# Seven block products in both SwiGLU stages, adaLN blocks on GpSimd and ScalarE, and x loaded first

## The reference

```python
# block 1
mod = silu(c) @ ada_w + ada_b                 # 1024 -> 6*1024, "adaLN": shifts, scales, gates
h = modulate(rmsnorm(x, norm1_g), shift1, scale1); proj = h @ w_in    # two attentions, branches, MLP
# block 2, layer A (l = 0): short convolution, then the first SwiGLU stage
# shared keys and values (w_ada_kv), layer B (l = 1): forgetting attention, then the second SwiGLU stage
mod_l = silu(c_2) @ w_ada_2[l] + b_ada_2[l]
y = (silu(h @ gate[l]) * (h @ up[l])) @ down[l]      # gate, up: 1024 x 2816, down: 2816 x 1024
x = layer_norm(alpha * x + gate_mod * y)
```

## Time and profile before

| | us |
|---|---|
| median of 3 runs | 1952.1 |
| the profiled execution's own time | 1950.68 |
| its span | 1948.9 |
| TensorE busy | 1888.5 (97%) |
| VectorE / ScalarE / GpSimd busy | 1291.9 / 814.6 / 466.0 |

### The profile page before, as it was taken

One profiled execution on the slowest core, in us unless ns is written; L12 is line 12 of the kernel. 1 busy time (PEld: TensorE's weight loads), 2 busy tenths in 40 slices (PEclk: granted clock), 3 DMA queues, 4 the chain that ended last, 5 costly groups with the idle time before them and its releaser, 6 DMA issues.

```text
span 1948.9 us, 23971 instructions
## 1 busy us (share of the span) xinstructions
PE 1888.5 (97%) x9600; PEld 1593.4 (82%) x9600; DVE 1291.9 (66%) x1969; ACT 814.6 (42%) x1238; POOL 466.0 (24%) x379
## 2 busy tenths in 40 slices
PE   4999999999999999999999999999999999999997
PEld 3788888887888887888788888877899778999996
DVE  6687655567667645665665555466677676777797
ACT  4677622352222235222522222248677553433333
POOL 4333210121111112001300000025643142445352
PEclk9999999999999999999999999999999999999998
DMA  9522366356565523542455442313211223323331
GB/s 334 153 85 66 113 222 238 120 193 238 211 221 201 188 87 117 186 151 93 168 201 187 173 151 87 108 65 130 71 58 52 87 72 101 109 95 101 108 100 52
DMA packets 134432, 267.65 MB, mean 137 GB/s; under 512 B 4576, under 2 KB 49648, under 8 KB 134321
## 3 DMA queue, kind: packets, MB, share of 16 engines
q1 hardware_dynamic: 129360, 248.59, 37.2%
q0 software_dynamic: 4960, 17.53, 2.5%
HBM read 261.84 MB, written 8.45 MB: 139 GB/s over the span
## 4 chain that ended last, share of the span: by engine, by line
PE 68%; DVE 3%; ACT 3%; POOL 2%; issue 1%; DVEq 0%; POOLq 0%; ACTq 0%
PE ps L720 22%; PE ps L722 21%; PE ps L721 21%; PE ps L880 1%; ACT t L1400 1%; ACT t L1396 1%; PE ps L869 1%; PE ps L858 0%; POOL t L2722 0%; PE ps L897 0%; PE ps L898 0%; PE ps L896 0%; DVE t L1889 0%; DVE t L1874 0%; POOL t L2531 0%
## 5 line engine op out<-in xcount | busy, mean ns | idle before, releaser
L720 PE MATMUL ps<-t 128*128 128x512 f32 (+1 forms) x2720 | 997.0, 367 | 12.1 <-POOL t L2626 5.2
L722 PE MATMUL ps<-t 128*128 128x512 f32 (+1 forms) x2720 | 989.6, 364 | 0.0
L721 PE MATMUL ps<-t 128*128 128x512 f32 (+1 forms) x2720 | 985.8, 362 | 0.0
L720 PEld LDWEIGHTS ps<-t 128*128 128x128 f32 x2720 | 513.2, 189 | 95.3 <-POOL t L2531 5.8
L722 PEld LDWEIGHTS ps<-t 128*128 128x128 f32 x2720 | 512.7, 189 | 84.6
L721 PEld LDWEIGHTS ps<-t 128*128 128x128 f32 x2720 | 513.1, 189 | 79.8 <-issue 1.0
L1810 DVE TENSOR_TENSOR t<-t 128x2048 fp32r<-128x2048 f32 x115 | 267.2, 2323 | 315.7 <-ACT t L1347 315.5
L1347 ACT ACTIVATE t<-t 128x2048 fp32r<-128x2048 f32 x115 | 219.7, 1911 | 465.2 <-PE ps L722 457.6
L1822 DVE CUSTOM_DVE_ANT_0 t<-t 128x1024 f32<-128x1024 f32 x144 | 174.8, 1255 | 6.8 <-DMA t<-in_adakv_t 3.6
L1874 DVE SCALAR_TENSOR_TENSOR t<-ps,t 128x512 f32<-128x512 f32 x184 | 131.7, 748 | 71.4 <-PE ps L722 68.1
L2531 POOL TENSOR_TENSOR t<-t 128x512 fp32r<-128x512 f32 x88 | 115.5, 1330 | 197.1 <-ACT t L1354 196.5
(11 more groups left out here) (196 smaller groups left out, 1894.7 us busy)
## 6 DMA issues: line engine op xcount, KB each, us to landing
t<-in_ada SPq DMA_DIRECT2D x48, 1024.0 KB, 5.9
t<-in_gate SPq DMA_DIRECT2D x22, 1024.0 KB, 5.2
t<-in_up SPq DMA_DIRECT2D x22, 1024.0 KB, 5.2
t<-in_down SPq DMA_DIRECT2D x22, 1024.0 KB, 5.1
t<-in_w_in SPq DMA_DIRECT2D x17, 1024.0 KB, 5.7
t<-in_w_mlp_in SPq DMA_DIRECT2D x16, 1024.0 KB, 5.3
t<-in_w_mlp_out SPq DMA_DIRECT2D x16, 1024.0 KB, 5.1
t<-in_ada_t POOLq DMA_DIRECT2D x13, 1024.0 KB, 6.2
```

The costliest lines, as they stand in the source:

```text
L720: pe.matmul(o, wh, xh, start=first, stop=False)
L721: pe.matmul(o, wh, xl, start=False, stop=False)
L722: return pe.matmul(o, wl, xh, start=False, stop=last)
```

## The change

1. The stage of l = 0 gets the same plan as that of l = 1: `plan_ffn2(l)` for both, 18 "S" slots each. In both stages gate and up slots now alternate, so that one gate tile and one up tile (128x1024 each) do, and the third sums buffer is `spare_b` in place of `csb[1]`. h4 is kept whole (`h4_all`), as h6 was.
2. adaLN blocks 61 to 79 are multiplied by GpSimd (`ada_product`, one 128x2048 `tensor_tensor` each, behind `weight_sums(n + 1)` in its queue) and summed by ScalarE (`ada_sum`, two 128x1024 `Copy` with an accumulator, ahead of the `first product` of the next step). They have two buffers. They fall on slots 75, 76, 77, 79, 80, 81, 83, 84, 85, 87, 88, 89, 91, 92, 93, 95, 96, 97 and 99. The S slots are 79 to 82, 85 to 88, 91 to 94, 97 to 99 and 101 to 103.
3. At the start x is loaded ahead of adaLN blocks 0 and 4; the squares and their sums go ahead of the rest on ScalarE and VectorE; the units of slots 0 and 1 wait for single pieces, and GpSimd does `low(0)` and `low(1)` after two pieces of slot 0.

```diff
+    for w, what in ((gate, "gate"), (up, "up")):
+        for p in range(2):
+            plan_role("A", w, 512 * p, 0, l, what, 0, p)
+    for f in range(4):
+        for p in range(2 if f else 0):
+            plan_role("S", gate, 0, 512 * f + 256 * p, l, "gate", f, p)
+            plan_role("S", up, 0, 512 * f + 256 * p, l, "up", f, p)
+        for hf in range(2):
+            plan_role("A", down, 512 * f, 512 * hf, l, "down", f, hf)
+    plan_role("S", gate, 0, 2560, l, "gate", 4, 0)
+    plan_role("S", up, 0, 2560, l, "up", 4, 0)
+    plan_role("S", gate, 0, 2048, l, "gate", 5, 0)
+    plan_role("C", down, 2560, 0, l, "down4", 4, 0)
+    plan_role("S", up, 0, 2048, l, "up", 5, 0)
+    plan_role("S", gate, 0, 2304, l, "gate", 5, 1)
+    plan_role("S", up, 0, 2304, l, "up", 5, 1)
...
+ADA_FFN = stream_ada()
+for _j in range(ADA_FFN, len(ADA)):
+    _i = _j - ADA_FFN
+    _at = AT_FFN + 2 + _i * 24 // (len(ADA) - ADA_FFN - 1)
+    ADA_BUF[_j] = ("ffn", _i % 2)
+    ADA_LOADS.setdefault(_at - 1 if _i > 1 else AT_FFN, []).append(_j)
+    ADA_SUMS.setdefault(_at, []).append(_j)
...
 (job_unit, TensorE)
+                if n < 2:
+                    on.wait_ge(w_lo_p, "slot", n, u // 2)
+                elif u == 0:
+                    slot_lo(on, n)
                 if u == 0:
-                    slot_lo(on, n)
                     claim(bank)
...
 (ScalarE, start)
-            for i, bank in enumerate((0, 4)): ... row copies
             on.wait_ge(d_cols, "eps")
             for k in range(KT):
                 square("n1", k, x_in[k // 4], "landed")
+            for i, bank in enumerate((0, 4)): ... row copies
+            root("n1", False, rmse)
             for c in range(4):
                 piece(0, c)
-            root("n1", False, rmse)
...
 (ScalarE, ffn2)
+                def ada_sum(j):
+                    on.wait_ge(p_ada, "product", j)
+                    col = ADA[j][2]
+                    for i in range(2):
+                        v = ada_buffer(j)[:, i * D:(i + 1) * D]
+                        ins = act.activation(v, v, ACT.Copy, accum_out=mods[:, col + i:col + i + 1])
+                    ins.then_inc(a_ada.sem, a_ada.up("sum", j))
...
 (VectorE, start)
+            for k in range(1, KT):
+                add("n1", k)
             ada_sum(0)
+            roots("n1", False)
             ada_sum(4)
             two_columns(0)
-            for k in range(1, KT):
-                add("n1", k)
-            roots("n1", False)
...
 (GpSimd)
+            def ada_product(j):
+                on.wait_ge(ada_landed(j), "landed", j)
+                v = ada_buffer(j).rearrange("p (a k) -> p a k", a=2)
+                c = csb[ADA[j][3]][:, :].rearrange("p (a k) -> p a k", a=1).broadcast_to([P, 2, D])
+                pool.tensor_tensor(v, v, c, ALU.mult).then_inc(p_ada.sem, p_ada.up("product", j))
+
             def ffn2(l, site):
-                take(33)
+                for n in sorted(n for n in ROLE if ROLE[n][0] == l):
+                    slot[0] += 1
+                    if in_products(n + 1):
+                        weight_sums(n + 1)
+                    for j in ADA_SUMS.get(n, ()):
+                        ada_product(j)
...
 (SyncE, start)
             sp.dma_start(csb[0][:, :], a["c_b"]).then_inc(c_in[0].sem, c_in[0].up("landed", by=16))
-            ada_load(0)
-            ada_load(4)
             for hf in range(2): ... x
+            ada_load(0)
+            ada_load(4)
             load(0)
```

More of the change, by code:

```diff
@@ L1084, in ffn2, with hidden, down4 @@
+            def ffn2(l, site, h):
+                def hidden(k):
+                    return hidden_t[l][:, 0, k % 4, :], hidden_t[l][:, 1, k % 4, :]
+                def down4():
+                    n = take("C", f"down{l}", 2560, 0)
+                    slot_lo(on, n)
+                    hi, lo = slot_view(WH, n), slot_view(WL, n)
+                    for hf in range(2):
                         for kt in range(2):
-                            xh, xl, ready = act_of(4)(kt)
-                            for signal, event in ready:
-                                on.wait_ge(signal, *event)
@@ L1488, in program_act @@
             act.activation(ada_mem["start"][7][:, 0:D], csb[0][:, :], ACT.Sigmoid).then_inc(a_norm.sem, a_norm.up("silu", 0))
+            on.wait_ge(d_cols, "eps")
+            for k in range(KT):
+                square("n1", k, x_in[k // 4], "landed")
             for i, bank in enumerate((0, 4)):
@@ L2627, in low @@
                     p_lo.sem, p_lo.up("h1", k))
-            for c in range(4):
+            for c in range(2):
                 piece(0, c)
-            for k in range(4):
+            for k in range(2):
+                low(k)
+            for c in (2, 3):
+                piece(0, c)
+            for k in (2, 3):
                 low(k)
@@ L2800, in ada_load @@
                 if before:
-                    on.wait_ge(d_ada, "sum", before[-1])
+                    ada_summed(on, before[-1])
                 elif j == 7:
```

845 lines of the change are left out of this document (347 added, 498 removed).

## The result

The changed kernel took 1975.4 us (median of 4 runs, 1973.57 to 1981.82), the kernel before beside it 1952.7 (1949.6 to 1953.83): a ratio of 1.012, 95% interval 1.010 to 1.015. The profiled executions differ by the same amount, 1971.8 against 1948.9 us.

What follows compares the result with a forecast made beforehand. TensorE, busy 1888.5 of 1948.9 us, was taken to bound the kernel. 1950.7 - 16.8 (S slots) - 8.5 (start) + 19.6 (product stalls) = 1945.0, a median of about 1946 us, range 1926 to 1965.

Steps and rivals of the forecast that it cites:

- rival B: Stage of l = 0: excess of 4.4 us paid in all 11 slots, 48 us; time 1965 to 1985; chance 0.22.
- the walk: Slots 79 to 82 followed with taken durations and turns: stalls 1.8, 4.3, 1.2 us, 7.9 with a late `raw_lo`.
- S slots, -16.8: Stage of l = 0: 18 S slots save 16.8 us, by comparing both stages before the change.
- Stage of l = 1, nothing: Stage of l = 1: the sum held no term for it, so no change was counted.
- Start, -8.5: Kernel start: x loaded first and single pieces end slot 0 8.5 us earlier; bounds 5.2 and 10 us.
- Rival C: Start gives back 3 us or less, as VectorE's sums set its end; time 1952; chance 0.08.
- Products, +19.6: S slots of l = 0: GpSimd's products make TensorE stall 19.6 us together; bounds 0 and 48 us.
- Clock, 0 in the sum: Clock drop after TensorE's stalls: 1.7 us after one wait, 10 for six, not counted in the sum.
- rival D: Stalls of 24 to 29 us, as the clock falls in each group: no change that can be told; chance 0.09.
- Products on down slots cost nothing: Down and plain slots: products are free, 6.5 us of cover against 4.6; 2.7 would show with a second turn.
- Whether it is one exclusive turn: VectorE instructions with both inputs in SBUF and GpSimd's never overlap; the holder keeps its turn; 2.30 in place of 1.23 us.
- Rival A: S slots: GpSimd's product yields or has more slack, so products are hidden; 1927, up to 1931 us; chance 0.21.

Runs made afterwards that it cites:

- no_product: Changed kernel without GpSimd's 19 products, the adaLN blocks summed by ScalarE as loaded: 1940.3 us, ratio 0.994 to the kernel before.
- shifts_early: Changed kernel with VectorE's shifts and fox columns one slot earlier, as the kernel before had them: 1971.2 us, ratio 1.008 to the kernel before.
- shifts_late: Changed kernel with VectorE's shifts 4 to 7 and fox columns moved to the first of the two last down slots: 1974.0 us.
- start_alone: Kernel before with only the changed kernel's start: 1946.6 us, ratio 0.997 to the kernel before.
- half_product: Changed kernel with all 19 products multiplying only the first half of their block (128x1024): 1951.9 us, ratio 0.999 to the kernel before.
- down_dve: Changed kernel with VectorE summing the 19 adaLN blocks itself, in plain, down and C slots only: 1998.6 us, ratio 1.023 to the kernel before.
- spread: Changed kernel with 6 more blocks summed by VectorE in the conv stage, 13 products outside S slots, shifts one slot earlier: 1967.3 us.
- placed: Changed kernel with 9 more blocks summed by VectorE in the conv stage, 10 products outside S slots, loads one slot ahead, shifts earlier: 1941.2 us.

## Why the prediction was wrong

The forecast was 1946, inside 1926 to 1965; 1975.4 came out, where rival B stood (1965 to 1985, chance 0.22). The prediction says that its range leaves out the upper part of B; it leaves out all of it. B has the time right by luck more than by its mechanism: it asked for 38 to 58 us of stalls and clock, paid in all 11 slots, and 34.0 came, in fewer; the rest of its time comes from the S slots' term and the stage of l = 1, which B took over unchanged. The mechanism of the stalls, GpSimd's turn, was named, and the walk found most of their places. The sum failed in its sizes: three terms (S slots, start, products) were off to the same side, and two (the stage of l = 1, the clock) stood at nothing.

- **S slots, -16.8.** The steps are as said: slot 79 begins at 999.01 and slot 80 at 1008.99, 9.98 us. But the stage without products is 353.63, not 346.69: 6.9 are missing, so -9.9. The wait of 4 us ahead of step 24 of slot 104 and the half clock behind it (1.7) are most of it, and both stand in no_product too. The step that failed is the comparison of the two stages of the kernel before: it took over a length that belongs to another order of the last slots.
- **Stage of l = 1, nothing.** No term stood in the sum; it cost 4.0. The new order of roles in the last slots was in the diff and was not costed. Shifts and columns were not followed past `second` and `third` on VectorE. shifts_early gives 2.4 of it back, shifts_late 3.2.
- **Start, -8.5.** It brought 6.5 in the change's profile and 6.5 in the medians of start_alone, within its bounds of 5.2 to 10. The square that needs x's second half starts at 12.05 in place of 10.6, straight behind its landing; from there the 5.0 us to VectorE's last sum hold (17.0 in place of 15.6). ScalarE's modulation starts at 24.14 in place of 21.8, the first unit comes at 27.17 in place of 24.8, and `convert(2)`, which ends slot 0, at 51.94 in place of 49.7 (58.27 before): 2.2 us short of the 8.5, about as at the first unit. start_alone shows that the term stands by itself. Rival C falls.
- **Products, +19.6, the step that decided.** They cost 34.0. The duration was right: 4.62 us at the least, against 4.6 taken. The waits were mostly right in place: those for `sums_lo` in slots 81, 82, 88, 93 and 94 at steps 36 and 60, as forecast, and one more in 87. In size: slots 79 to 83 6.9 against 7.9, slots 91 to 94 5.8 against 7.9, but slots 85 to 89 7.1 against 3.8 and slots 97 to 100 4.3 against 0 (gaps between TensorE's matmuls, less their usual step). Together 24.1, with 19.6 forecast. That the first group agrees is partly luck: at slot 81 the gap is 3.5 where the walk had 1.8, at slot 82 1.8 where it had 4.3. The walk let a product start when the sums ahead of it were done, and began each group of S slots with GpSimd free. Both fail. The product of slot 85 ran at 1082.1, in slot 86 (from 1080.95), which the walk had free of products, without any wait for its block: the product of slot 84 and the sums behind it came first ("Which products"). The one of slot 99 ran at 1245.6, in slot 100, because GpSimd waited 8.1 us for its block; in all it waited for a landing in 8 cases of 19, 80.3 us, most of them in plain and down slots.
- **Clock, 0 in the sum.** With products TensorE is busy 21.7 us at 0.50, without them 3.4: some 9 us. The prediction knew the price (1.7 us after one stall of 1.75) and put it into rivals B and D, but left it out of the forecast although it counted stalls of 1.8 and 4.3 us there. 19.6 with 8 to 10 of clock would have been rival D, no change; here the failed step is that a price which had been read was left out of the sum.
- **Products on down slots cost nothing.** Alone, nearly: 3.3 us for eight, 2.3 of it one wait for `convert` at the start of slot 76, and 0.7 at slot 104, where the half clock lasts 6.8 us in that profile in place of 3.4. Together with the products of the S slots, no: the eight add 387.6 - 378.5 = 9.1 us there.
- **Whether it is one exclusive turn.** Yes. `sums_lo` of 4.99 us in place of 1.22, and the join with a PSUM input of 0.68 in the middle of a product. Rival A falls. The Trainium skill's rule (SBUF — State Buffer, "SBUF: two separate sides") speaks of such a lock, and this trace agrees: 4.99 in place of 1.22.

Put together: -6.5 for the start, -9.9 for the S slots, +34.0 for the products, +4.0 for l = 1, +1.4 between the stages (its cause was not looked for), -0.2 at the end: +22.8 of the 22.9 us.

What is open: why two thirds of the products' price go with the last 2.3 us of their hold is argued from the slack of 4.3 and 7.1 us and fits half_product, but the chain of each wait was not replayed. The part of the 4.0 us in the stage of l = 1 that neither placing of the shifts gives back (0.8 to 1.6) has no experiment of its own. And no run has the products in shorter pieces without the adaLN sum ahead of `first product`.

## What to carry to other kernels

An idle share alone does not say whether an engine can take more work. GpSimd, busy 148 of 347 us in a stage of S slots, could not take 4.6 us more per slot without VectorE's next instruction being late. Cutting the product into pieces took most of that lateness away and brought it back through ScalarE's queue, which waited for the last piece; moving 10 of the products to slots where nobody waits, and 9 blocks to a stage where VectorE had room, is what helped. Before a forecast is summed, give each stall its clock, and follow every instruction that a reordering moves on the engine that is nearly late. And a block for an in-order queue must have landed when its turn comes: down_dve and spread were 57 and 26 us slower than placed, and their traces show late blocks ahead of their longest waits.
